# The gate projection as eight groups of split products ahead of the attention's units

## The chip, the cores and the metric

The kernel runs on one core of one Trainium2 chip. The metric is the device time of one execution in microseconds (us). Engines are called TensorE (PE in the profile; PEld are its weight loads), VectorE (DVE), ScalarE (ACT), GpSimd (POOL) and SyncE (SP); the last one here only issues DMA transfers.

## What is computed

A two-layer trunk over 512 positions of width 1024, in float32: a gMLP mixer and a mixture of experts (MoE), then shared keys and values, then a forgetting attention and a second MoE. The change touches the attention alone:

```python
def forgetting_attention(h, k, v, cum, w_qg, q_norm, w_out):
    q, gate = jnp.split(h @ w_qg, 2, axis=-1)
    q = rmsnorm(q.reshape(B, S, N_HEADS, HEAD_DIM), q_norm)
    ...
        s = jnp.einsum('bqhd,bkhd->bhqk', q[:, q0:q1], kb).astype(jnp.float32) * scale
        decay = cum[:, :, q0:q1, None] - cum[:, :, None, :q1]
        s = jnp.where(mask, s + decay, -jnp.inf)
        p = jax.nn.softmax(s, axis=-1)
        outs.append(jnp.einsum('bhqk,bkhd->bqhd', p.astype(vb.dtype), vb))
    ...
    return (o * jax.nn.sigmoid(gate)) @ w_out
```

`h` is 512 x 1024; query and gate are 1024 wide each, 16 heads of 64. The sigmoid is computed as a tanh of half the argument, with the factors folded in elsewhere.

## The kernel before

Every engine has a program written out by hand, in order, and the engines meet at semaphores. Weights of the dense projections come as 20-odd tiles of 1024 rows x 512 columns (2 MB) through a ring of two buffers in `EB[1]`: `load_tile(i)` on SyncE (line 317) waits until the groups of products that read tile i-2 are done. A dense projection is made of *split products* (`split_product`, lines 1067 to 1069): both operands are split into a rounded high part and the rest, and three matmuls (high x high, high x low, low x high) of type float32r take the place of one float32 matmul. The weight tile is split by ScalarE (line 528, high part, four pieces) and VectorE (line 753, low part, in place). One *group* is the 8 x 3 matmuls that fill a PSUM bank of 128 x 512; it increments `acc_ready`. `project_heads` makes the 8 query groups (tiles T_Q, T_Q+1), in banks 0 and 1, and turns normalised heads (`turn_heads`, line 1296) behind each next group; the last turn, `turn_heads(15)`, came alone.

The attention then runs in 32 *units*: 8 pairs of heads (c), each with 4 query blocks of 128 (i), keys up to (i+1) x 128 wide. On TensorE a unit u is: scores of two heads (line 1374) and the mask (1377) into banks 0/1 or 2/3; a quarter of the gate projection of this pair; every fourth unit the output product of the pair before (1402), 16 matmuls; the transposes of the probabilities of unit u-2 (1413). The gate's quarter is two plain float32 products of 128 x 128 by 128 x 512 (line 1389) into bank 7, with raw weights from the ring and with `hT`, which VectorE restores as the sum of the two halves (line 1005) in the first four units. Each float32 product appears as two MATMUL records. `g_done` counts a pair's gate; ScalarE applies tanh (line 696) into `GT` and counts `g_out`.

VectorE in unit u: adds the decay row and takes the maximum for two heads (line 1015; the first needs the row buffers `nck`), reciprocal (1024) and scaling (1028) of unit u-1, copy of the first head's transposes of unit u-2 (1034), and after a pair's output product the gating and its split (1040 to 1042). ScalarE: two exponentials (687), copy of the second head's transposes (705). The row buffers `nck` are loaded by ScalarE's queue (line 674), two pairs at first and then one pair at a time, two pairs ahead.

TensorE's transposes of a unit wait for VectorE's scaling of that unit and for both copies of the unit before it; the scores wait for the maxima two units back; the output product waits for the last copies of its pair and for `o_gated` of the pair before.

Of the kernel before, what the change touches and what calls it, by code (L numbers as in the profile page):

```python
# [24 lines left out]
P = 128  # L25
D = 1024
T = 512
NT = T // P
# [25 lines left out]
def trunk(nc, x_in, a_norm, a_w_in, a_b_in, a_v_norm, a_w_s, a_b_s, a_w_out, kv_norm, kv_w, kv_b_f, k_norm,  # L54
          b_norm, b_w_qg, q_norm, b_w_out, m_norm, m_w_group, m_b_group, m_w_expert, m_b_expert,
          m_w1, m_w3, m_w2, out):
    with ExitStack() as ctx:
# [177 lines left out]
        v_out = sem("v_out")  # L235
        g_done = sem("g_done")
        g_out = sem("g_out")
# [41 lines left out]

        G_V, G_U, G_K, G_VV, G_Q, G_WO = 0, 16, 32, 40, 48, 56  # L280


        def split_no(i):
            return i if i < T_G else i - (T_WO - T_G)


        H_LO = {"a": 0, "kv": 2 * NT, "b": 4 * NT}
        H_BACK = 6 * NT

# [15 lines left out]
        def _(sp):  # L305
            def load_tile(i):
                if i >= 2:

                    j = i - 2
                    if T_O <= j < T_K:  # L310
                        sp.wait_ge(out_done, 4 * (j - T_O + 1))
                    elif j >= T_G:
                        sp.wait_ge(g_done, 4 * (j - T_G + 1))
                    else:
                        groups = 4 * (j + 1 if j < T_O else j + 1 - (T_K - T_O))
                        sp.wait_ge(acc_ready, groups)
                sp.dma_start(ring[i % 2], tiles[i]).then_inc(tile_loaded[i % 2], 16)
# [174 lines left out]
        def _(act):  # L492
# [177 lines left out]
            act.dma_start(ncum_rows, junk[0:HEADS, 0:T]).then_inc(ncum_stored, 16)  # L670
            head_norms(1, G_Q, 1, QT, {1: T_Q + 1})
            def load_nck(c):
# [9 lines left out]
            for u in range(PAIRS * NT + 2):  # L682
                if u < PAIRS * NT:
# [6 lines left out]
                    if u % NT == NT - 1 and u // NT + 2 < PAIRS:  # L690
                        load_nck(u // NT + 2)
                if u < PAIRS * NT and u % NT == NT - 1:

                    c = u // NT
                    act.wait_ge(g_done, c + 1)
                    a.activation(GT[:, c, :], ps[7][:, :], ACT.Tanh, scale=0.5).then_inc(g_out, 1)

                q = u - (PAIRS // 2 * NT + 2)
# [13 lines left out]
        def _(dve):  # L712
# [282 lines left out]
            then(v.tensor_scalar(kq_gain[:, 1:2], kq_gain[:, 1:2], DH ** -0.5, None, ALU.mult))  # L995
            head_norms(1, G_Q, {1: T_Q + 1})
            n_units = PAIRS * NT
            for u in range(n_units + 4):
                if u < n_units:
                    i, c = u % NT, u // NT  # L1000
                    w = (i + 1) * P
                    if c == 0:

                        dve.wait_ge(acc_ready, G_Q + 8)
                        v.tensor_tensor(hT[:, 2 * i:2 * i + 2, :], hT_hi[:, 2 * i:2 * i + 2, :].bitcast(F32),  # L1005
                                        hT_lo[:, 2 * i:2 * i + 2, :].bitcast(F32), ALU.add).then_inc(h_lo, 1)
                    if i == 0:
                        dve.wait_ge(nck_loaded[c % 2], 32 * (c // 2 + 1))
                    for h in range(2):
                        dve.wait_ge(s_done, 2 * u + h + 1)  # L1010
                        if u >= 3:

                            dve.wait_ge(pt_tr, 2 * (u - 3) + h + 1)

                        v.tensor_tensor_reduce(out=Pr[:, u % 3, h, 0:w], in0=ps[2 * (u % 2) + h][:, 0:w],
                                               in1=nck[:, c % 2, h, 0:w], scale=-1.0, scalar=BIG, op0=ALU.add,
                                               op1=ALU.min, accum_out=nmx[:, u % 3, h:h + 1]).then_inc(s_max, 1)
# [44 lines left out]
        def _(pe):  # L1062
# [51 lines left out]

            def project_transposed(i, g0, bank_free):

                for j in range(4):
                    g = g0 + j
                    bank_free(g)
                    for k in range(KD):  # L1120
                        wait_split(i, k, j == 0)
                        last = split_product(ps[g % 2][:, :], w_part(i % 2, k, j * P, (j + 1) * P), h_part(k),
                                             k == 0, k == KD - 1)
                    last.then_inc(acc_ready, 1)

            def router_step(l, t):
# [233 lines left out]
            project_heads("b", T_Q, G_Q, 1, free_q)  # L1360
            turn_heads(15)


            pe.wait_ge(kn_out, 16)
            n_units = PAIRS * NT
            for u in range(n_units + 3):
                if u < n_units:
# [8 lines left out]
                    for h in range(2):  # L1376
                        mm(ps[2 * (u % 2) + h][:, i * P:w], ident_b[:, :], mask_b[:, :], start=False, stop=True)\
                            .then_inc(s_done, 1)

                    j = T_G + c // 4  # L1380
                    if i == 0:
                        pe.wait_ge(tile_loaded[j % 2], 16 * (j // 2 + 1))
                        if c >= 1:
                            pe.wait_ge(g_out, c)
                    if c == 0:

                        pe.wait_ge(h_lo, H_BACK + i + 1)
                    for k in range(2 * i, 2 * i + 2):
                        last = mm(ps[7][:, :], ring[j % 2][:, k, c % 4 * P:(c % 4 + 1) * P], hT[:, k, :],  # L1389
                                  start=k == 0, stop=k == KD - 1)  # L1390
                    if i == NT - 1:
                        last.then_inc(g_done, 1)
                if u >= 3 and (u - 3) % NT == NT - 1:
# [4 lines left out]
                    if c >= 1:  # L1398
                        pe.wait_ge(o_gated, c)
                    for b in range(NT):  # L1400
                        for h in range(2):
# [52 lines left out]
```

## Time and profile before

| | us |
|---|---|
| median of 3 runs | 1839.46 |
| lowest, highest | 1835.39, 1840.23 |
| span of the profiled execution | 1838.5 |
| TensorE busy | 1706.3 (93%) |
| VectorE busy | 640.1 (35%) |
| ScalarE busy | 378.6 (21%) |

The page shows one execution; times in it run from the span's start. Busy times are unions of records, and a matmul's record reaches past the start of the next one, so the rate of a stream of matmuls is read from starts, not from lengths. "Idle before, releaser" says how long an engine stood still before a row and who ended that. Shares over the whole span mix stages; the stage in question is 1062 to 1211.

### The profile page before, as it was taken

Reading aid. Unit: us, or ns where it says so; the run is one execution under the profiler, and the core shown is the slowest. Engines: PE = TensorE matmul, PEld = TensorE weight load, DVE = VectorE, ACT = ScalarE, POOL = GpSimd, SP = SyncE. Lnnn points to the kernel's source line nnn. Section 1 sums busy time; section 2 is a strip of 40 time slices with the busy share of each in tenths; the row PEclk is TensorE's granted clock in tenths of the full one; section 3 lists DMA queues with packets and bytes.
Section 4 is the critical chain, followed back from the end, with each engine's and each line's share of the span. In section 5 each row is a group of like instructions: output and inputs, shape, how many; then the busy total and the mean of one; then the engine's idle time right before and its main releaser. Section 6 shows DMA issues by size and latency. Waiting matters only on the chain.

```text
span 1838.5 us, 22412 instructions
## 1 busy us (share of the span) xinstructions
PE 1706.3 (93%) x8401; PEld 882.0 (48%) x8402; DVE 640.1 (35%) x1174; ACT 378.6 (21%) x685; POOL 35.3 (2%) x62
## 2 busy tenths in 40 slices
PE   6999998899999999997699989987999999999993
PEld 4888887333333333332587844465333333333331
DVE  5336523322222222223725346734322222222223
ACT  5441312011111111111441334512111111111110
POOL 2000000000000000000000000000000000000001
PEclk8999999899999999998789999988999999999997
DMA  5652227799999779994223122055799797999964
GB/s 185 210 183 90 93 92 290 296 405 427 429 428 428 308 299 417 430 416 132 81 92 102 48 80 81 24 227 230 305 424 427 315 389 320 417 427 430 429 271 148
DMA packets 64254, 497.62 MB, mean 271 GB/s; under 512 B 5760, under 2 KB 5872, under 8 KB 39120
## 3 DMA queue, kind: packets, MB, share of 16 engines
q1 hardware_dynamic: 52256, 461.39, 61.6%
q10 hardware_dynamic: 7920, 22.58, 3.3%
q0 software_dynamic: 4032, 13.01, 2.2%
q8 instruction: 32, 0.52, 0.1%
q14 instruction: 14, 0.11, 0.0%
HBM read 468.61 MB, written 28.34 MB: 270 GB/s over the span
## 4 chain that ended last, share of the span: by engine, by line
PE 49%; issue 45%; DVE 4%; DMA 1%; ACT 1%; POOL 1%; POOLq 0%; ACTq 0%; DVEq 0%
PE ps L1193 13%; PE ps L1176 7%; PE ps L1208 7%; PE ps L1067 6%; PE ps L1069 6%; PE ps L1068 6%; DVE SCR L845 1%; PE ps L1183 1%; DVE SCR L735 1%; PE ps L1263 1%; DMA EB<-y_rows,pos_i 1%; DVE X L865 1%; PE ps L1337 1%; POOL EB L450 1%; PE ps L1090 0%
## 5 line engine op out<-in xcount | busy, mean ns | idle before, releaser
L1193 PE MATMUL ps<-EB,SCR 128*64 128x512 f32 x2176 | 478.6, 592 | 2.9 <-DVE SCR L828 2.9
L1193 PEld LDWEIGHTS ps<-EB,SCR 128*64 128x64 f32 x2176 | 157.2, 137 | 311.7 <-issue 308.4
L1176 PE MATMUL ps<-H,SCR 128*64 128x512 f32 x1120 | 255.2, 598 | 7.2 <-DVE SCR L780 7.2
L842 DVE TENSOR_TENSOR SCR<-SCR,ps 64x512 f32<-64x512 f32 x68 | 46.9, 690 | 605.2 <-ACT SCR L566 605.2
L1208 PE MATMUL ps<-EB,SCR 128*64 128x512 f32 x1088 | 248.5, 598 | 0.0
L1069 PE MATMUL ps<-EB_r 128*128 128x512 f32 x512 | 202.4, 395 | 0.0
L572 ACT ACTIVATE SCR<-ps 64x512 f32 (+1 forms) x136 | 80.6, 593 | 545.4 <-PE ps L1208 487.5
L1176 PEld LDWEIGHTS ps<-H,SCR 128*64 128x64 f32 x1120 | 81.9, 138 | 167.7 <-issue 167.7
L1208 PEld LDWEIGHTS ps<-EB,SCR 128*64 128x64 f32 x1088 | 72.5, 136 | 127.6 <-issue 127.6
L1067 PE MATMUL ps<-EB_r,H_r 128*128 128x512 f32 x320 | 129.5, 405 | 1.4 <-DVE EB L882 0.9
L1068 PE MATMUL ps<-EB_r,H_r 128*128 128x512 f32 x320 | 127.4, 398 | 0.0
L1068 PE MATMUL ps<-EB_r 128*128 128x512 f32 x320 | 125.1, 391 | 0.0
L566 ACT ACTIVATE SCR<-ps 64x512 f32<-64x512 f32 x68 | 40.1, 589 | 363.0 <-PE ps L1193 363.0
L753 DVE TENSOR_TENSOR EB_r<-EB,EB_r 128x1024 fp32r<-128x1024 f32 x80 | 92.8, 1220 | 46.9 <-ACT EB_r L528 46.9
L1069 PEld LDWEIGHTS ps<-EB_r 128*128 128x128 f32 x512 | 98.2, 192 | 21.2
L845 DVE COPY SCR<-ps 128x512 f32<-128x512 f32 x68 | 47.0, 692 | 141.7 <-PE ps L1176 141.7
L528 ACT ACTIVATE EB_r<-EB 128x1024 fp32r<-128x1024 f32 x80 | 78.3, 1047 | 82.2 <-DMA EB<-in_a_w_out 44.0
L1067 PE MATMUL ps<-EB_r 128*128 128x512 f32 x192 | 75.7, 394 | 2.0 <-DVE EB_r L1042 2.0
L1389 PE MATMUL ps<-H,EB 128*128 128x512 f32 x128 | 64.3, 625 | 6.4 <-DVE H L1005 5.7
L1067 PEld LDWEIGHTS ps<-EB_r,H_r 128*128 128x128 f32 x320 | 62.1, 194 | 14.9 <-DVE EB L882 1.3
L1068 PEld LDWEIGHTS ps<-EB_r,H_r 128*128 128x128 f32 x320 | 61.9, 193 | 12.6
L1068 PEld LDWEIGHTS ps<-EB_r 128*128 128x128 f32 x320 | 60.5, 189 | 12.6
(199 smaller groups left out, 1377.3 us busy)
## 6 DMA issues: line engine op xcount, KB each, us to landing
EB<-in_m_w SPq DMA_DIRECT2D x192, 2048.0 KB, 10.2
y_rows<-SCR ACTq DMA_DIRECT2D x68, 256.0 KB, 7.5
EB<-in_a_w_in SPq DMA_DIRECT2D x8, 2048.0 KB, 10.4
y_rows<-X SPq DMA_DIRECT2D x4, 2048.0 KB, 14.6
EB<-in_a_w_out SPq DMA_DIRECT2D x4, 2048.0 KB, 7.9
EB<-in_kv_w SPq DMA_DIRECT2D x4, 2048.0 KB, 10.3
EB<-in_b_w_qg SPq DMA_DIRECT2D x4, 2048.0 KB, 10.3
SCR<-ncum_rows ACTq DMA_DIRECT2D x16, 256.0 KB, 3.6
```

The costliest lines, as they stand in the source:

```text
L528: a.activation(ring_hi[j][:, 2 * q:2 * q + 2, :], ring[j][:, 2 * q:2 * q + 2, :], ACT.Copy)\
L572: a.activation(ysb[0:CAP, bass.ds((n & 1) * D + h * COL, COL)], ps[4][h * CAP:(h + 1) * CAP, :], ACT.Copy).then_inc(m["y_out"], 1)
L753: v.tensor_tensor(ring_lo[j][:, 2 * q:2 * q + 2, :], ring[j][:, 2 * q:2 * q + 2, :], ring_hi[j][:, 2 * q:2 * q + 2, :].bitcast(F32), ALU.s ...
L842: v.tensor_tensor(hid[0:CAP, :], silu[CAP:P, :], ps[0][CAP:P, :], ALU.mult).then_inc(m["hid"], 1)
L845: v.tensor_copy(xg, ps[1][:, :]).then_inc(m["xg"], 1)
L1067: mm(o, left[0], right[0], start=start, stop=False)
L1068: mm(o, left[0], right[1], start=False, stop=False)
L1069: return mm(o, left[1], right[0], start=False, stop=stop)
L1176: last = mm(ps[1][h * CAP:(h + 1) * CAP, :], S[:, c, :], H[:, c * D + h * COL:c * D + (h + 1) * COL], start=c == 0, stop=c == NT - 1)
L1193: last = mm(ps[0][h * CAP:(h + 1) * CAP, :], xT[:, k, :], w[:, k, :], start=k == 0, stop=k == KD - 1)
L1208: last = mm(ps[4][h * CAP:(h + 1) * CAP, :], hidT[:, k, :], w2_sb[s][:, k, h * COL:(h + 1) * COL], start=k == 0, stop=k == KE - 1)
L1389: last = mm(ps[7][:, :], ring[j % 2][:, k, c % 4 * P:(c % 4 + 1) * P], hT[:, k, :], start=k == 0, stop=k == KD - 1)
```

## The change

The gate projection leaves the units. It is made of split products like the others, eight groups (`G_G`) in banks 6 and 7 in turn, right behind the query projection, with the last turn of the query heads behind its first group. Its two weight tiles are split by ScalarE and VectorE: the first within `head_norms` at its sixth group, the second by ScalarE behind the first tanh and by VectorE behind `head_norms`. ScalarE's eight tanh stand one behind the other ahead of the first load of `nck`. The sum that restored `hT` is gone from VectorE. SyncE's loads of the two output-projection tiles now wait for gate groups 4 and 8 (`acc_ready`) in place of `g_done`. The first output product waits once for all eight tanh.

```diff
-                    elif j >= T_G:
-                        sp.wait_ge(g_done, 4 * (j - T_G + 1))
                     else:
                         groups = 4 * (j + 1 if j < T_O else j + 1 - (T_K - T_O))
                         sp.wait_ge(acc_ready, groups)
...
-            head_norms(1, G_Q, 1, QT, {1: T_Q + 1})
+            head_norms(1, G_Q, 1, QT, {1: T_Q + 1, 5: T_G})
+            for c in range(PAIRS):
+                act.wait_ge(acc_ready, G_G + c + 1)
+                a.activation(GT[:, c, :], ps[6 + c % 2][:, :], ACT.Tanh, scale=0.5).then_inc(g_out, 1)
+                if c == 0:
+                    split_tile(T_G + 1)
+
...
-                if u < PAIRS * NT and u % NT == NT - 1:
-
-                    c = u // NT
-                    act.wait_ge(g_done, c + 1)
-                    a.activation(GT[:, c, :], ps[7][:, :], ACT.Tanh, scale=0.5).then_inc(g_out, 1)
-
...
-            head_norms(1, G_Q, {1: T_Q + 1})
+            head_norms(1, G_Q, {1: T_Q + 1, 5: T_G})
+            split_tile(T_G + 1)
...
-                    if c == 0:
-
-                        dve.wait_ge(acc_ready, G_Q + 8)
-                        v.tensor_tensor(hT[:, 2 * i:2 * i + 2, :], hT_hi[:, 2 * i:2 * i + 2, :].bitcast(F32),
-                                        hT_lo[:, 2 * i:2 * i + 2, :].bitcast(F32), ALU.add).then_inc(h_lo, 1)
...
-            turn_heads(15)
-
+
+            def free_g(g):
+                c = g - G_G
+                if c >= 2:
+                    pe.wait_ge(g_out, c - 1)
+
+            pe.wait_ge(ncum_ready, 1)
+            project_transposed(T_G, G_G, free_g, 6, lambda: turn_heads(15))
+            project_transposed(T_G + 1, G_G + 4, free_g, 6)
...
-                    j = T_G + c // 4
-                    if i == 0:
-                        pe.wait_ge(tile_loaded[j % 2], 16 * (j // 2 + 1))
-                        if c >= 1:
-                            pe.wait_ge(g_out, c)
-                    if c == 0:
-
-                        pe.wait_ge(h_lo, H_BACK + i + 1)
-                    for k in range(2 * i, 2 * i + 2):
-                        last = mm(ps[7][:, :], ring[j % 2][:, k, c % 4 * P:(c % 4 + 1) * P], hT[:, k, :],
-                                  start=k == 0, stop=k == KD - 1)
-                    if i == NT - 1:
-                        last.then_inc(g_done, 1)
...
+                    else:
+                        pe.wait_ge(g_out, PAIRS)
```

TensorE's order around an output product, before (L1374 scores, L1377 mask, L1389 gate, L1402 output product, L1413 transposes):

```order
L1413 MATMUL ps<-ident,SCR 128x128 x8
L1374 MATMUL ps<-EB 128x384 x2
L1377 MATMUL ps<-mask_b,ident_b 128x128 x2
L1389 MATMUL ps<-H,EB 128x512 x2
L1402 MATMUL ps<-EB 64x512 x2
L1402 MATMUL ps<-EB 64x384 x2
L1402 MATMUL ps<-EB 64x256 x2
L1402 MATMUL ps<-EB 64x128 x2
L1413 MATMUL ps<-ident,SCR 128x128 x2
L1374 MATMUL ps<-EB 128x512 x2
L1377 MATMUL ps<-mask_b,ident_b 128x128 x2
L1389 MATMUL ps<-H,EB 128x512 x2
```

The same place after (L1375 scores, L1378 mask, L1391 output product, L1402 transposes):

```order
L1402 MATMUL ps<-ident,SCR 128x128 x8
L1375 MATMUL ps<-EB 128x384 x2
L1378 MATMUL ps<-mask_b,ident_b 128x128 x2
L1391 MATMUL ps<-EB 64x512 x2
L1391 MATMUL ps<-EB 64x384 x2
L1391 MATMUL ps<-EB 64x256 x2
L1391 MATMUL ps<-EB 64x128 x2
L1402 MATMUL ps<-ident,SCR 128x128 x2
L1375 MATMUL ps<-EB 128x512 x2
L1378 MATMUL ps<-mask_b,ident_b 128x128 x2
```

The gate's rows are gone; scores, output product, transposes and the next scores now follow one another directly.

ScalarE's order between the last query heads and the first exponentials, before (L641, L643 head norms, L655 turned heads out, L674 row loads, L687 exponentials):

```order
L641 ACTIVATE SCR<-ps 128x512
L643 ACTIVATE hr<-hss,eps 128x8
L655 ACTIVATE EB<-ps,cols 128x4x128 x2
L674 DMA SCR<-ncum_rows 128x512 x4
L687 ACT_TABLE_LOAD
L687 ACTIVATE SCR,rsum<-SCR,nmx 128x128 x2
```

The same place after (L637, L639, L651 the heads; L670 tanh; L524 split of the second gate tile; L676 row loads; L689 exponentials):

```order
L637 ACTIVATE SCR<-ps 128x512
L639 ACTIVATE hr<-hss,eps 128x8
L651 ACTIVATE EB<-ps,cols 128x4x128 x2
L670 ACT_TABLE_LOAD
L670 ACTIVATE EB<-ps 128x512
L524 ACTIVATE EB_r<-EB 128x1024 x4
L670 ACTIVATE EB<-ps 128x512 x7
L676 DMA SCR<-ncum_rows 128x512 x4
L689 ACTIVATE SCR,rsum<-SCR,nmx 128x128 x2
```

The row loads and the exponentials now stand behind the eight tanh and a tile's split.

## Rows read from the trace of the kernel before

**Rows 1.** The page, part 1: busy us, share of the span, instructions.
```profile
PE 1706.3 (93%) x8401; PEld 882.0 (48%) x8402; DVE 640.1 (35%) x1174; ACT 378.6 (21%) x685; POOL 35.3 (2%) x62
```

**Rows 2.** The windows view: stretch, length, busy us (instructions) per engine, granted clock.
```profile
core 0: us, PE busy (x) PEld busy (x) DVE busy (x) ACT busy (x) POOL busy (x), PEclk, DMA share, GB/s
1062.80:1074.10 11.30, 4.20 (x22) 1.89 (x20) 2.72 (x5) 3.26 (x5) 0.00 (x0) 1.00 0.85 274
1074.10:1087.80 13.70, 11.87 (x34) 4.86 (x34) 9.63 (x30) 5.60 (x19) 0.00 (x0) 0.75 0.03 10
1087.80:1200.70 112.90, 111.01 (x538) 53.91 (x536) 75.03 (x251) 53.33 (x154) 0.00 (x0) 1.00 0.15 49
1200.70:1210.90 10.20, 5.88 (x24) 3.23 (x24) 3.96 (x9) 4.49 (x5) 0.00 (x0) 0.67 0.59 204
```

**Rows 3.** The timeline, TensorE, one pair of units: start, length, what.
```profile
1112.75 2.38 PE L1402 MATMUL ps<-EB 128*64 128x512 f32 x16
1115.06 0.44 PE L1413 MATMUL ps<-ident,SCR 128*128 128x128 f32 x2
...
1116.61 1.94 PE L1389 MATMUL ps<-H,EB 128*128 128x512 f32 x4
1118.38 0.60 PE L1413 MATMUL ps<-ident,SCR 128*128 128x128 f32 x4
...
1128.60 2.37 PE L1402 MATMUL ps<-EB 128*64 128x512 f32 x16
```

**Rows 4.** The same pair, VectorE, where it waited: idle before, releaser.
```profile
1115.43 0.29 DVE L1034 COPY EB<-ps 128x128 f32<-128x128 f32 x1 [2.62 <-PE ps L1413]
1116.76 0.69 DVE L1015 CUSTOM_DVE_ANT_0 SCR<-ps,SCR 128x512 f32<-128x512 f32 x1 [1.04 <-PE ps L1377]
...
1123.17 0.42 DVE L1015 CUSTOM_DVE_ANT_0 SCR<-ps,SCR 128x256 f32<-128x256 f32 x1 [0.24 <-PE ps L1377]
...
1125.43 0.69 DVE L1034 COPY EB<-ps 128x512 f32<-128x512 f32 x1 [0.89 <-PE ps L1413]
1126.88 0.56 DVE L1015 CUSTOM_DVE_ANT_0 SCR<-ps,SCR 128x384 f32<-128x384 f32 x1 [0.75 <-PE ps L1377]
```

**Rows 5.** The timeline in the u projection, TensorE, 24 split matmuls apart.
```profile
214.02 0.39 PE L1067 MATMUL ps<-H_r,EB_r 128*128 128x512 f32 x1
...
219.46 0.39 PE L1067 MATMUL ps<-H_r,EB_r 128*128 128x512 f32 x1
```

**Rows 6.** The chain that ended last, two turns of heads in the key stage.
```profile
937.92 0.44 PE ps L1296 x4
...
943.86 0.44 PE ps L1296 x4
```

**Rows 7.** The timeline between query projection and units, four engines and queues.
```profile
1062.61 0.54 SPq L317 DMA_DIRECT2D EB<-in_b_w_qg  x1
...
1065.28 0.66 PE L1296 MATMUL ps<-ident,SCR 128*128 128x128 f32 x4 [2.27 <-DVE SCR L960]
...
1066.75 2.12 ACTq L674 DMA_DIRECT2D SCR<-ncum_rows  x4
...
1074.10 0.29 DVE L1015 CUSTOM_DVE_ANT_0 SCR<-ps,SCR 128x128 f32<-128x128 f32 x1 [7.74 <-DMA SCR<-ncum_rows]
```

**Rows 8.** Landing of the row loads: all sixteen; two at 1134, beside a tile load.
```profile
DMA to landing us min/median/max: 3.0/3.6/7.1
...
SCR<-ncum_rows ACTq DMA_DIRECT2D x2, 256.0 KB, 4.6
```

**Rows 9.** Groups by line, 1062 to 1210: count, busy us, mean ns, idle before.
```profile
L753 DVE TENSOR_TENSOR EB_r<-EB,EB_r 128x1024 fp32r<-128x1024 f32 x4 | 4.9, 1220 | 0.0
...
L696 ACT ACTIVATE EB<-ps 128x512 f32<-128x512 f32 x8 | 4.7, 592 | 0.0
```

**Rows 10.** The windows view in steps of 8 us, columns as in rows 2.
```profile
1072.00:1080.00 8.00, 4.20 (x6) 1.67 (x8) 4.03 (x13) 1.97 (x8) 0.00 (x0) 0.69 0.23 89
1264.00:1272.00 8.00, 2.72 (x60) 2.32 (x56) 3.85 (x17) 2.58 (x4) 0.00 (x0) 0.85 1.01 428
```

More of the change, by code:

```diff
@@ L235, in trunk @@
         v_out = sem("v_out")
-        g_done = sem("g_done")
         g_out = sem("g_out")
@@ L278, in trunk @@
         T_V, T_U, T_O, T_K, T_VV, T_Q, T_G, T_WO = 0, 4, 8, 12, 14, 16, 18, 20
-        G_V, G_U, G_K, G_VV, G_Q, G_WO = 0, 16, 32, 40, 48, 56
+        G_V, G_U, G_K, G_VV, G_Q, G_G, G_WO = 0, 16, 32, 40, 48, 56, 64
         def split_no(i):
-            return i if i < T_G else i - (T_WO - T_G)
+            return i
         H_LO = {"a": 0, "kv": 2 * NT, "b": 4 * NT}
-        H_BACK = 6 * NT
         TURN = {"a": 3, "kv": 3, "b": 2}
@@ L1113, in project, with project_transposed @@
                     last.then_inc(acc_ready, 1)
-            def project_transposed(i, g0, bank_free):
+            def project_transposed(i, g0, bank_free, bank=0, after_first=None):
                 for j in range(4):
@@ L1121, in project_transposed @@
                         wait_split(i, k, j == 0)
-                        last = split_product(ps[g % 2][:, :], w_part(i % 2, k, j * P, (j + 1) * P), h_part(k),
+                        last = split_product(ps[bank + g % 2][:, :], w_part(i % 2, k, j * P, (j + 1) * P), h_part(k),
                                              k == 0, k == KD - 1)
                     last.then_inc(acc_ready, 1)
+                    if after_first is not None and j == 0:
+                        after_first()
             def router_step(l, t):
```

## The prediction

> **What bounds the kernel now.** I read the page's first part: TensorE is busy 93% of the span [rows 1], so it bounds the kernel nearly everywhere. The change touches one stage, so I cut that stage out with the windows view [rows 2]. From the end of the query projection to the first unit's maximum, 1062.8 to 1074.1: TensorE 4.2 us busy of 11.3. Attention units, 1087.8 to 1200.7: TensorE 111.0 of 112.9, VectorE 75.0, ScalarE 53.3. Tail, 1200.7 to 1210.9, when the output projection starts.
>
> In the steady units (pairs c, four units i = 0..3 each; "T(i)" the transposes of unit i, "S(i)" its scores, "O" the pair's output product) the timeline of TensorE gives the make-up of one pair [rows 3]: O starts at 1112.75 and again at 1128.60, so a pair takes 15.85 us. The gate holds TensorE from 1116.61 to the next T at 1118.38, 1.77 us, and much the same in the other three units: about 7.2 us. What is left, O (2.31) with the S, their masks and the T, is 8.6.
>
> VectorE's timeline of the same pair [rows 4] is the one to read for what comes next. It waits five times: 2.62 (copy of T(0), behind O), 1.04 (scores 512 wide), 0.24, 0.89 and 0.75, in all 5.54. So it works 15.85 - 5.54 = 10.31 us a pair, more than TensorE without the gate: the bound changes hands.
>
> **The gate ahead of the units (added).** 64 split products of three matmuls each. The same form stood in the u projection: 24 matmuls from 214.02 to 219.46, 5.44 us a group [rows 5]. Eight groups: 43.5 us, plus the turn of the last query heads that now falls behind the first group, about 0.4: 44 us, from 1062.8 to 1106.8, all on the path. The wait in which TensorE sat idle for that turn (2.27 us, [rows 7]) is hidden by the first group; it lies inside the 11.3 us that I replace below, so it is not counted again.
>
> Both tiles must be split in time. The first one loads when four query groups are done, as now, and is split at the sixth group; the key stage did just that (a tile split at the same place) and its turns stayed 5.94 us apart, 937.92 to 943.86 [rows 6], so I price it at nothing. The second is issued at 1062.61 [rows 7]; give it 11 us to land, to 1073.6. ScalarE and behind it VectorE split it in four pieces, 1.22 each on VectorE, 4.9 in all [rows 9]: ready by about 1079, wanted at 1085. If that cover went, each us of lateness would be one on the path. Banks 6 and 7 need tanh two groups back; tanh of the second group waits behind that split, to about 1078.9, and TensorE asks for it at 1079.6. It holds by less than a us.
>
> **The first maximum (a wait moved and lengthened).** The row buffers of the decay are loaded by ScalarE, and this issue now stands behind all eight tanh. Behind it are queued the first exponentials; VectorE's first maximum waits for the data, and TensorE, after two units' scores, for VectorE. The last gate group ends at 1106.8; who waits for it moves 0.2 later, as SyncE's issue at 1062.61 behind the last query group of 1062.4 [rows 7], one tanh is 0.59 [rows 9], so the issue comes at 1107.6 to 1107.7. Before, from the issue at 1066.75 to the first maximum at 1074.10 took 7.35 us [rows 7], beside the 2 MB tile load of 1062.61. Lower bound: the second row's issue, 0.45 after the first, and the median landing of 3.6 [rows 8], so 1111.8. Upper: 7.35 again, 1115.1. A tile load stands beside it again, since the last tile is issued when the last gate group frees its buffer, but it no longer has a lead of 4 us. A pair of row loads issued with such a load beside it landed in 4.6 [rows 8]. I take 1113.7, **39.6 us later** than 1074.10.
>
> What the Trainium skill says of it (page "DMA: Bandwidth & Descriptors", section on queues, rings and completion order): a DMA engine takes the rows it has work for in turn, a packet at a time. By that rule both transfers share from the start, and by it the start would lie in the upper half of my bounds, 1 us later at most.
>
> **The gate out of the units (removed).** With 7.2 us of TensorE gone the pair does not fall to TensorE's 8.6. Take VectorE's work, 10.31, and ask which waits stay.
> - 0.24, 0.89, 0.75: VectorE waited for scores or transposes that stood behind a gate product. Without it TensorE has them ready. Gone.
> - 1.04: from T(0)'s start, 1115.06, S(3) follows at once, and the 512-wide scores reach VectorE at 1116.76; the gate is not in this chain. Stays.
> - 2.62: O starts once the copies of the 512-wide T(3) are out, then 2.31 of O and 0.37 of T(0) must pass before the copy of T(0). VectorE began unit 2's maxima at 1126.88 - 15.85 = 1111.03 and had work until 1115.43 - 2.62 = 1112.81 [rows 4]: 1.78. O, held back by a gate product, began only 1.72 after those maxima, at 1112.75. Now it begins as soon as the copies are out, about 0.25 after them, and the copy of T(0) can start 0.25 + 2.31 + 0.37 = 2.93 after them. 2.93 - 1.78 = 1.15 stays. S(2) stands in the same queue and adds about 0.15.
> A pair: 10.31 + 1.04 + 1.15 + 0.15 = **12.65, say 12.7**. Bounds: 10.3 (no wait) and 14.0 (10.31 + 2.62 + 1.04).
>
> Sum from the first maximum to the output projection. First pair, 1074.10 to 1087.8 [rows 2]: 13.7 now. After: VectorE's work without the steps that the first units skip is some 6.5, and the waits for S(2) and S(3) at the lower clock, which follows the idle stretch, about 2.5: 9, with 7 and 12 as ends. Seven pairs: 112.9 now; 7 x 12.7 = 88.9, plus the split of the output tile, four pieces of 1.22 on VectorE [rows 9], of which one falls in the 1.15 wait: +3.7, together 92.6. Tail: 10.2 both times [rows 2]; its chain of copies, O and gating has no gate product. So 136.8 becomes 9 + 92.6 + 10.2 = 111.8, **25.0 us less**. Tanh and the sum of the two query-side halves (L1005) leave the units too; ScalarE waits there anyway, and the latter lies in the first pair.
>
> Net: +39.6 - 25.0 = +14.6. The output projection and the MoE behind it start that much later with their loads issued by the same releases, so nothing is won back. The profiled span of 1838.5 lies 1.0 under the median of the runs; 1838.5 + 14.6 + 1.0 = **1854**.
>
> **Rivals.**
> (1) TensorE's clock. It now would be busy two thirds of a pair with gaps of 2 us, and the first pair begins after 5 to 6 idle us. Before, after such a stretch, the granted clock was 0.69 in the window from 1072 [rows 10], that is for part of it 1.2 GHz instead of 2.4, and over the first pair 0.75 [rows 2]; it rose when TensorE had been dense. Against: a window with TensorE 2.72 busy of 8 had 0.85 [rows 10]. If it stays low through the units, TensorE needs 2 x 8.6 = 17.2 a pair, 4.5 over my 12.7, in seven pairs +31: **1885**; if half the time, 1870. The Trainium skill ("TensorE: Matmul & The Clock Gate", section on PSUM-queue depth-cycling) describes it: frequent micro-idles between groups of matmuls made the clock go up and down. By that rule the time would be that of this rival.
> (2) VectorE never waits: a pair costs 10.3, the sum falls by 7 x 2.4 = 16.8: **1837**, no change. It decides where O and S(3) hide behind VectorE's work; against it stands the order of O, T(0), S(3) on TensorE.
> (3) Faster: the units stay TensorE's and fall to its own 8.6 a pair: 7 x 4.1 = 29 less than my sum, **1825**. The break-even is a pair of 12.7 - 14.6/7 = 10.6, and faster by 0.3% needs under 9.8. VectorE's measured work of 10.31 excludes it, unless a part of it is waiting that the trace shows as work.
>
> **How the numbers follow.** 0.3% is 5.5 us, about what measurement tells from no change. Forecast, 12 to 14 us a pair and the first maximum within its bounds: 1848 to 1865, chance 0.74. Clock rival 0.14, from 1865 to 1885. VectorE without waits 0.09, 1837 to 1845. Faster 0.03. The range takes in the forecast and the nearer side of both neighbours: 1845 to 1868. Faster 0.03, same 0.09, slower 0.88.
>
> **What would show it.** In the profile of the changed kernel: TensorE full from 1062.8 to about 1107, in groups of 5.44; then idle till a first VectorE maximum near 1114, with a DMA as releaser; pairs 12.7 apart, O to O, with VectorE waiting about 1.0 before the 512-wide maximum and 1.2 before the copy of T(0), and hardly elsewhere; clock 1.00 from the second pair on; output projection at 1225 or so. I am wrong if pairs take under 11.3 (waits were mis-read), over 14 (clock), or if the groups of the gate stall for a tile.

## The result, and the profile after

| | before | changed |
|---|---|---|
| median of four runs, us | 1838.75 | 1864.78 |
| lowest, highest | 1835.39, 1840.23 | 1863.42, 1865.98 |
| span of the profiled execution | 1838.5 | 1861.6 |
| mean granted clock of TensorE | 0.963 | 0.954 |
| output projection starts at | 1210.9 [rows 2] | 1234.6 |

The changed kernel is slower: ratio 1.0141, 95% interval 1.0127 to 1.0156, or 26.0 us. The forecast was 14.6 us slower. The time lies inside the range, but more than 10 us above the forecast, and that difference is what most of the experiments are about.

The page's first part of the changed kernel, to be held against [rows 1]:

```profile
PE 1710.4 (92%) x8465; PEld 904.0 (49%) x8466; DVE 644.0 (35%) x1178; ACT 385.8 (21%) x693; POOL 34.8 (2%) x62
```

TensorE is busy 4 us longer, which says nothing of the 23. The output projection starts 23.7 us later than before, and the span is 23.1 us longer: the whole change lies in this one stage. Here is the stage in the windows view, with the columns of [rows 2]; the stretches are the gate, the idle stretch behind it, the first pair up to the first row of steady work, the other units, and the tail.

```profile
core 0: us, PE busy (x) PEld busy (x) DVE busy (x) ACT busy (x) POOL busy (x), PEclk, DMA share, GB/s
1062.80:1107.10 44.30, 44.30 (x200) 36.47 (x198) 6.21 (x7) 11.41 (x16) 0.00 (x0) 1.00 0.29 95
1107.10:1115.40 8.30, 1.64 (x13) 0.83 (x12) 0.04 (x1) 0.60 (x1) 0.00 (x0) 0.85 0.82 260
1115.40:1122.70 7.30, 5.48 (x24) 2.35 (x24) 6.11 (x27) 4.99 (x18) 0.00 (x0) 0.70 0.38 138
1122.70:1224.10 101.40, 78.95 (x420) 42.77 (x420) 74.57 (x252) 48.66 (x146) 0.00 (x0) 0.77 0.10 32
1224.10:1234.60 10.50, 6.35 (x24) 3.48 (x24) 3.81 (x7) 4.63 (x6) 0.00 (x0) 0.61 0.11 27
```

The gate is as forecast: 44.3 us, TensorE busy in all of it, clock 1.00. In the fourth stretch TensorE is busy 78% where it had been busy 98%, VectorE only 74%, and the granted clock is 0.77 where [rows 2] had 1.00. So no engine is full there, and the clock is low.

The timeline of the same kernel from the end of the gate, four engines and queues (start, length, what, idle before and releaser); it answers to [rows 7]:

```profile
1107.28 0.38 SPq L313 DMA_DIRECT2D EB<-in_b_w_out  x1
1107.29 0.60 ACT L670 ACTIVATE EB<-ps 128x512 f32<-128x512 f32 x1 [4.84 <-PE ps L1061]
1107.35 2.02 ACTq L676 DMA_DIRECT2D SCR<-ncum_rows  x4
...
1115.36 0.29 DVE L1007 CUSTOM_DVE_ANT_0 SCR<-ps,SCR 128x128 f32<-128x128 f32 x1 [36.42 <-DMA SCR<-ncum_rows]
1115.92 1.65 PE L1375 MATMUL ps<-EB 64*128 64x384 f32 x4 [7.18 <-DVE nmx L1007]
...
1234.61 0.50 PE L1059 MATMUL ps<-EB_r 128*128 128x512 f32 x1 [1.97 <-DVE EB_r L1034]
```

The row loads are issued at 1107.35, 0.07 us behind a 2 MB tile load, and the first maximum comes 8.0 us after the issue. TensorE stands idle for 7.18 us.

TensorE's timeline in one pair of the changed kernel, from one output product to the next; it answers to [rows 3]:

```profile
1128.09 2.38 PE L1391 MATMUL ps<-EB 128*64 128x512 f32 x16
...
1132.90 0.29 PE L1378 MATMUL ps<-mask_b,ident_b 128*128 128x128 bf16 x2
1134.74 0.84 PE L1402 MATMUL ps<-ident,SCR 128*128 128x128 f32 x6 [1.55 <-DVE EB L1026]
1135.52 0.70 PE L1375 MATMUL ps<-EB 64*128 64x256 f32 x4
1136.15 0.28 PE L1378 MATMUL ps<-mask_b,ident_b 128*128 128x128 bf16 x2
1138.40 1.94 PE L1402 MATMUL ps<-ident,SCR 128*128 128x128 f32 x8 [1.97 <-DVE EB L1026]
1140.27 1.65 PE L1375 MATMUL ps<-EB 64*128 64x384 f32 x4
1141.86 0.39 PE L1378 MATMUL ps<-mask_b,ident_b 128*128 128x128 bf16 x2
1142.18 3.07 PE L1391 MATMUL ps<-EB 128*64 128x512 f32 x16
```

The same two groups of instructions before, where no gap stood ahead of them:

```profile
1124.79 1.04 PE L1413 MATMUL ps<-ident,SCR 128*128 128x128 f32 x8
1125.76 0.92 PE L1374 MATMUL ps<-EB 64*128 64x384 f32 x4
```

This is the heart of the result. A pair takes 14.09 us, not 12.7. TensorE waits twice, 1.55 us ahead of T(2) and 1.97 us ahead of T(3), each time for VectorE's copies. In this pair T(3), behind the second gap, takes 1.94 us where it took 1.04, the scores 384 wide 1.65 for 0.92, and the output product 3.07 for 2.38. Per 8 us the windows view shows it as clock 1.00 and then 0.57:

```profile
1128.00:1136.00 8.00, 6.45 (x46) 3.40 (x44) 5.84 (x19) 3.46 (x10) 0.00 (x0) 1.00 0.16 45
1136.00:1144.00 8.00, 6.04 (x25) 3.00 (x24) 5.88 (x24) 4.16 (x14) 0.00 (x0) 0.57 0.06 23
```

This pair does not stand for all of them. In five of the eight pairs the clock is low already at T(2), which then takes 1.08 to 1.51 us where it takes 0.84 at full clock. Two of the five:

```profile
1163.75 1.20 PE L1402 MATMUL ps<-ident,SCR 128*128 128x128 f32 x6 [1.55 <-DVE EB L1026]
...
1208.41 1.47 PE L1402 MATMUL ps<-ident,SCR 128*128 128x128 f32 x6 [1.55 <-DVE EB L1026]
```

So the low level begins near either gap, once in each pair.

VectorE's waits around the end of that pair, to be held against [rows 4]:

```profile
1142.18 0.56 DVE L1007 CUSTOM_DVE_ANT_0 SCR<-ps,SCR 128x384 f32<-128x384 f32 x1 [1.96 <-PE ps L1378]
...
1145.55 0.29 DVE L1026 COPY EB<-ps 128x128 f32<-128x128 f32 x1 [1.59 <-PE ps L1402]
1146.88 0.69 DVE L1007 CUSTOM_DVE_ANT_0 SCR<-ps,SCR 128x512 f32<-128x512 f32 x1 [1.04 <-PE ps L1378]
```

Two of these were forecast, 1.15 and 1.04. The first, 1.96 for the slow T(3) and scores, was not. The product starts lie 14.09, 14.79, 14.12, 16.38, 14.29 and 13.90 us apart (the fourth pair holds the split of the output tile). Before they lay 15.84, 15.85, 15.83, 16.43, 15.84 and 15.75 apart.

### The profile page after: what moved, and what is told of

Same layout as the page of the kernel before. It is cut to its first block, busy times and chain, and to the rows that moved or that the text cites. A ratio compares the mean times of both kernels' runs of the same rounds, so it can differ in the third digit from the quotient of the medians.

```text
span 1861.6 us, 22546 instructions
## 1 busy us (share of the span) xinstructions
PE 1710.4 (92%) x8465; PEld 904.0 (49%) x8466; DVE 644.0 (35%) x1178; ACT 385.8 (21%) x693; POOL 34.8 (2%) x62
## 4 chain that ended last, share of the span: by engine, by line
PE 48%; issue 45%; DVE 4%; DMA 1%; ACT 1%; POOL 1%; POOLq 0%; ACTq 0%; DVEq 0%
PE ps L1187 13%; PE ps L1170 7%; PE ps L1202 7%; PE ps L1059 6%; PE ps L1061 6%; PE ps L1060 6%; DVE SCR L841 1%; PE ps L1177 1%; DVE SCR L731 1%; PE ps L1257 1%; DMA EB<-y_rows,pos_i 1%; DVE X L861 1%; PE ps L1331 1%; POOL EB L446 0%; PE ps L1082 0%
## 5 line engine op out<-in xcount | busy, mean ns | idle before, releaser
L1061 PE MATMUL ps<-EB_r 128*128 128x512 f32 x512 | 202.1, 395 | 0.0
L1060 PE MATMUL ps<-EB_r 128*128 128x512 f32 x384 | 150.0, 391 | 0.0
L749 DVE TENSOR_TENSOR EB_r<-EB,EB_r 128x1024 fp32r<-128x1024 f32 x88 | 102.1, 1220 | 56.2 <-ACT EB_r L524 56.1
L1061 PEld LDWEIGHTS ps<-EB_r 128*128 128x128 f32 x512 | 97.7, 191 | 20.9
L524 ACT ACTIVATE EB_r<-EB 128x1024 fp32r<-128x1024 f32 x88 | 86.0, 1047 | 81.0 <-DMA EB<-in_a_w_out 43.9
L1060 PEld LDWEIGHTS ps<-EB_r 128*128 128x128 f32 x384 | 72.5, 189 | 15.0
L1059 PE MATMUL ps<-EB_r 128*128 128x512 f32 x192 | 75.6, 394 | 2.0 <-DVE EB_r L1034 2.0
L1059 PE MATMUL ps<-H_r,EB_r 128*128 128x512 f32 x192 | 75.1, 391 | 0.0
L1061 PE MATMUL ps<-H_r,EB_r 128*128 128x512 f32 x192 | 74.7, 389 | 0.0
L1059 PEld LDWEIGHTS ps<-EB_r,H_r 128*128 128x128 f32 x320 | 61.9, 193 | 14.7 <-DVE EB L878 1.3
## 6 DMA issues: line engine op xcount, KB each, us to landing
EB<-in_m_w SPq DMA_DIRECT2D x192, 2048.0 KB, 10.2
EB<-in_b_w_qg SPq DMA_DIRECT2D x4, 2048.0 KB, 10.2
```

The lines of the kernel that those rows point to most:

```text
L524: a.activation(ring_hi[j][:, 2 * q:2 * q + 2, :], ring[j][:, 2 * q:2 * q + 2, :], ACT.Copy)\
L749: v.tensor_tensor(ring_lo[j][:, 2 * q:2 * q + 2, :], ring[j][:, 2 * q:2 * q + 2, :], ring_hi[j][:, 2 * q:2 * q + 2, :].bitcast(F32), ALU.s ...
L1059: mm(o, left[0], right[0], start=start, stop=False)
L1060: mm(o, left[0], right[1], start=False, stop=False)
L1061: return mm(o, left[1], right[0], start=False, stop=stop)
```

## The experiments

The theory: the sum is right at the full clock, and the lost clock in the units and the late rows make up the rest. The rivals: the chain between VectorE and TensorE is longer than read, so that pairs take 14 us at any clock; or the share of work on TensorE, not the gaps, sets the clock. Ratios are against the kernel before on the same chip, whose medians were 1838.71 for the first four kernels, 1839.23 for the next four and 1837.51 for the last two.

**Filler in both gaps.** Eight extra matmuls of type float32r, 128 x 512, stand ahead of T(2) and ahead of T(3) in each pair. They write into bank 7, which is free there, and nobody reads the result.

```diff
                 if 2 <= u < n_units + 2:
                     q = u - 2
                     i, c = q % NT, q // NT
+                    if u == 2:
+                        pe.wait_ge(g_out, PAIRS)
+                    if u % NT in (0, 1):
+                        for _ in range(8):
+                            mm(ps[7][:, :], hT_hi[:, 0, 0:P], hT_hi[:, 1, :], start=True, stop=True)
```

> The changed kernel, and in its attention units eight more float32r matmuls of 512 columns (8 x 0.227 = 1.8 us, results into free bank 7, read by nobody) ahead of the transposes in units 0 and 1 of every pair, where TensorE waits 2 us for VectorE's copies. Theory (lost clock): pairs took 14.3 us instead of the 12.7 forecast because the granted clock was 0.57 to 0.90; with the gaps filled it stays at 1.00, pairs fall to 12.7, and the whole is 8 to 11 us shorter than the changed kernel, 1854 to 1857. Rival (the recurrence was mis-sized, the clock is harmless): pairs stay at 14.3 or grow, time 1865 or more.

Measured: 1852.27 us (1848.68 to 1855.1), ratio 1.0077 (1.0057 to 1.0096). Extra work made the changed kernel 12.5 us faster, somewhat more than the 8 to 11 expected. Pairs: 12.38, 12.36, 12.38, 15.51, 12.38, 12.37. The windows view over the units of this kernel, and VectorE's waits in a pair:

```profile
1130.00:1218.00 88.00, 84.30 (x514) 51.71 (x512) 71.41 (x237) 45.32 (x136) 0.00 (x0) 1.00 0.10 31
```

```profile
1142.90 0.56 DVE L1007 CUSTOM_DVE_ANT_0 SCR<-ps,SCR 128x384 f32<-128x384 f32 x1 [0.38 <-PE ps L1378]
...
1145.52 0.29 DVE L1026 COPY EB<-ps 128x128 f32<-128x128 f32 x1 [0.85 <-PE ps L1407]
1146.85 0.69 DVE L1007 CUSTOM_DVE_ANT_0 SCR<-ps,SCR 128x512 f32<-128x512 f32 x1 [1.04 <-PE ps L1378]
```

The clock is 1.00 and the wait of 1.96 is down to 0.38. The three waits left come to 2.27 us; the forecast had 2.34 (1.04 + 1.15 + 0.15). A pair of 12.38 stands beside the forecast's 12.65. So the rival of a longer chain falls. The sum of the waits was right, its terms less so: 0.85 stands for 1.15, and 0.38 of a wait that the forecast called gone is still there.

From the first maximum (1117.29) to the output projection (1223.89) 106.6 us pass, 12.6 less than in the changed kernel. Of these 9.9 lie in the seven pairs (101.4 and 91.5 us) and 2.7 in the tail, which takes 7.8 us at clock 1.00. The kernel before had the tail at 10.2 us and 0.67 [rows 2], so part of what the filler wins is nothing that the change had lost.

**Half the filler** (four in place of eight, both places).

> As the run before with half the filling, four matmuls (0.9 us) at the same two places. Lost clock: it holds the clock in part, time between the changed kernel's 1865 and that of the full filling, some 1858 to 1862. Rival: no difference from 1865, or up to 1 us.

Measured: 1854.21 (1852.15 to 1855.45), ratio 1.0087 (1.007 to 1.0104). Pairs of 12.4 to 12.7, and 15.89 with the split; clock 0.98 in the units. The interval overlaps that of eight; I had expected a part of the gain, 1858 to 1862, and it came nearly whole.

**A quarter of it** (two, that is 0.45 us at each place).

> The changed kernel with two filling matmuls (0.45 us) at each of the two places in a pair, where four and eight gave pairs of 12.4 us at a clock of 1.00. If the clock follows how busy TensorE is, pairs lie between 12.4 and 14.3 and the time between 1854 and 1865, about 1860. If any filling is enough, 1854.

Measured: 1853.21 (1850.63 to 1854.81), ratio 1.0077 (1.0062 to 1.0092). Pairs: 12.37, 12.38, 12.37, 15.51, 13.13, 12.38. The windows view over the units, first this kernel, then the changed kernel without filler:

```profile
1128.00:1216.00 88.00, 67.22 (x424) 35.50 (x424) 71.56 (x237) 45.17 (x135) 0.00 (x0) 0.98 0.10 31
```

```profile
1128.00:1216.00 88.00, 68.26 (x364) 36.41 (x364) 64.65 (x215) 41.91 (x124) 0.00 (x0) 0.77 0.10 31
```

TensorE's busy share is the same or lower (67.2 against 68.3 of 88 us), and the clock is 0.98 against 0.77. That alone does not refute the rival of too little work, because slow matmuls count as busy for longer: this kernel did 424 matmuls in the 88 us, the other 364. It shows that the busy share cannot tell whether the clock holds. It also shows that the gaps need not be closed. They are only shorter, 1.03 and 1.45 us, and T(3) runs at full clock behind the second:

```profile
1146.97 0.85 PE L1407 MATMUL ps<-ident,SCR 128*128 128x128 f32 x6 [1.03 <-DVE EB L1026]
...
1150.63 1.06 PE L1407 MATMUL ps<-ident,SCR 128*128 128x128 f32 x8 [1.45 <-DVE EB L1026]
```

This kernel does not yet say which gap matters.

**Four in one gap only**, ahead of T(2) (unit 0 of the next pair, in the words of the expectation) or ahead of T(3) (unit 1). The first of the two edits, shown against the kernel with eight fillers:

```diff
-                    if u % NT in (0, 1):
-                        for _ in range(8):
+                    if u % NT in (0,):
+                        for _ in range(4):
```

> The changed kernel with four filling matmuls (0.9 us) in unit 0 of a pair alone: the amount per pair is that of two plus two, which kept pairs at 12.4, but the gap ahead of unit 1's transposes stays open. If the amount of work decides the clock, pairs stay at 12.4 and the time is near 1853. If each gap counts, that pair's clock falls again and the time lies at 1857 to 1865.

> The same four matmuls in unit 1 of a pair alone, the gap ahead of unit 0's transposes open. By amount: near 1853, as with the other place. If one of the gaps is the one that counts, this run and the one before differ, one near 1853 and one near 1860 or more.

Measured ahead of T(2): 1863.25 (1862.48 to 1863.6), ratio 1.0139 (1.0116 to 1.0163), no gain over the changed kernel; pairs 13.78, 14.1, 14.26, 17.28, 14.16, 14.16. Ahead of T(3), in `(1,)`: 1855.37 (1854.69 to 1858.89), ratio 1.0102 (1.0075 to 1.013), and pairs 12.76, 12.38, 12.37, 15.51, 12.37, 12.72. The units in the windows view, and TensorE's gap that was left, ahead of T(2) first:

```profile
1128.00:1216.00 88.00, 71.83 (x386) 37.80 (x384) 64.12 (x215) 42.00 (x126) 0.00 (x0) 0.83 0.09 31
```

```profile
1136.54 1.94 PE L1407 MATMUL ps<-ident,SCR 128*128 128x128 f32 x8 [1.97 <-DVE EB L1026]
```

and ahead of T(3):

```profile
1128.00:1216.00 88.00, 69.78 (x424) 38.95 (x421) 71.14 (x237) 45.43 (x135) 0.00 (x0) 0.93 0.09 31
```

```profile
1159.49 0.85 PE L1407 MATMUL ps<-ident,SCR 128*128 128x128 f32 x6 [1.55 <-DVE EB L1026]
```

The gap of 1.97 us, left alone, keeps the clock at 0.83, and T(3) at its slow 1.94 in three of seven pairs and partly slow in three more. The gap of 1.55 us, left alone, still goes with 0.93 and pairs of 12.4 to 12.8. The gap ahead of T(3) carries most of the loss (by the ratios 0.39 of the 0.54 per cent that four fillers in both gaps gave back; the interval of this run is wide, and its upper end reaches into that of the changed kernel). Here the rival "share of work" falls: these two kernels and the one with two fillers in each gap have the same four fillers in a pair, and their clocks are 0.83, 0.93 and 0.98.

Part of the difference is not in the clock but in what it slows. In the second kernel T(2) is sometimes slow too:

```profile
1199.74 1.06 PE L1407 MATMUL ps<-ident,SCR 128*128 128x128 f32 x6 [1.55 <-DVE EB L1026]
```

The pair in which this stands takes 12.72 us, 0.35 more than one at full clock; it shows again as a longer wait of VectorE at its end (0.73 for 0.38). In the first kernel the pair with the slow T(3) shown takes 13.78, 1.4 more. A low clock behind T(2) is nearly hidden behind VectorE's work, and one at T(3), the scores and O is not.

**The row loads ahead of the tanh.**

```diff
             head_norms(1, G_Q, 1, QT, {1: T_Q + 1, 5: T_G})
...
+            act.wait_ge(ncum_stored, 16)
+            act.wait_ge(kn_out, 16)
+            load_nck(0)
+            load_nck(1)
             for c in range(PAIRS):
                 act.wait_ge(acc_ready, G_G + c + 1)
...
-            act.wait_ge(ncum_stored, 16)
-
-            act.wait_ge(kn_out, 16)
-            load_nck(0)
-            load_nck(1)
             for u in range(PAIRS * NT + 2):
```

> The changed kernel with the first two pairs' row loads issued by ScalarE ahead of the eight tanh in place of behind them. Theory (the wait of 8 us before the first maximum is this queueing): first maximum about 0.8 us after the last gate group, at 1108 in place of 1115.4, no idle stretch of 7 us on TensorE, first pair at full clock: 8 to 10 us shorter, about 1856. Rival (the units are bound by something that starts later, or the gate's own splits suffer): under 4 us.

Measured: 1852.8 (1851.78 to 1854.1), ratio 1.0078 (1.0061 to 1.0095): 12.0 us less than the changed kernel, where 8 to 10 were expected. VectorE's first maximum in the timeline:

```profile
1108.84 0.29 DVE L1006 CUSTOM_DVE_ANT_0 SCR<-ps,SCR 128x128 f32<-128x128 f32 x1 [28.12 <-PE ps L1377]
```

It is 6.5 us earlier, and its releaser is now the scores and no longer a DMA. Pairs stay at 13.9 to 14.2 (16.36 with the split) and the clock of the units at 0.78, so this loss is separate from the clock's. In the profiled executions the output projection starts 9.8 us earlier (1224.80): 6.5 from the maximum and 3.3 behind it. Of the latter, 2.3 lie ahead of the first output product: from the first maximum to there it is 10.5 us at clock 1.00, where the changed kernel took 12.7 at 0.70 behind its idle stretch. The spans differ by 9.3 and the medians by 12.0; the rest is scatter between executions, since the profiled one is the fastest of its four in the changed kernel and the slowest of its four here.

**Both together**, rows ahead and eight fillers.

> Both edits at once. If the two losses are separate they add up: 16 to 20 us shorter than the changed kernel, 1845 to 1849, still slower than the kernel before by 6 to 10: that remainder is 44 us of gate ahead against what its absence saves in the units at full clock. Rival (either edit repairs the clock alone): 8 to 11 us shorter.

Measured: 1842.8 (1842.01 to 1846.13), ratio 1.0024 (1.0014 to 1.0034); pairs 12.38, clock 1.00, output projection at 1214.41. That is 22.0 of the 26.0 us back, nearly the 12.5 + 12.0 of the two alone. What is left is 4.1 us: the first maximum comes at 1108.42, 34.3 us later than before, and from there to the output projection it takes 106.0 us where it took 136.8, 30.8 less. The difference is 3.5. That is not yet the bare exchange of one place of the gate for the other, since the kernel before has neither its rows early nor a tail at full clock. Beside the kernel before with its first rows early (1833.41, below) this one is 9 to 10 us slower.

**The kernel before, four sums first.** All four sums that restore `hT` (L1005) stand ahead of the first maximum, in its wait for the rows.

```diff
-                    if c == 0:
-
-                        dve.wait_ge(acc_ready, G_Q + 8)
+                    if u == 0:
+                      dve.wait_ge(acc_ready, G_Q + 8)
+                      for i in range(NT):
                         v.tensor_tensor(hT[:, 2 * i:2 * i + 2, :], hT_hi[:, 2 * i:2 * i + 2, :].bitcast(F32),
                                         hT_lo[:, 2 * i:2 * i + 2, :].bitcast(F32), ALU.add).then_inc(h_lo, 1)
+                      i = 0
```

> The kernel before, with VectorE's four sums that restore the float32 rows (line 1005) all ahead of the first maximum instead of one in each of the first four units. VectorE waits 7.7 us there for the row loads anyway, and TensorE waited 5.75 us for the second sum and then ran its first pair at a clock of 0.75. Theory (that idle stretch and its clock cost 10 us in the kernel before, which no gate ahead is needed to win): 7 to 10 us faster than before, about 1830. Rival (the row loads bind the first pair anyway): within 3 us of before.

Measured: 1834.82 (1831.06 to 1838.53), ratio 0.998 (0.9971 to 0.9989), 4.4 us less than before. The first output product came at 1091.63 in place of 1096.91. The sign holds; I had expected 7 to 10.

**The kernel before, first rows early.** The halves of the row buffer are exchanged, so that the first pair's rows do not have to wait for the turned heads, and are loaded ahead of the query heads.

```diff
-            head_norms(1, G_Q, 1, QT, {1: T_Q + 1})
...
-                    act.dma_start(nck[:, c % 2, h, :], ncum_rows[2 * c + h].partition_broadcast(P))\
+                    act.dma_start(nck[:, (c + 1) % 2, h, :], ncum_rows[2 * c + h].partition_broadcast(P))\
...
             act.wait_ge(ncum_stored, 16)
+            load_nck(0)
+            head_norms(1, G_Q, 1, QT, {1: T_Q + 1})
...
             act.wait_ge(kn_out, 16)
-            load_nck(0)
             load_nck(1)
...
-                                               in1=nck[:, c % 2, h, 0:w], scale=-1.0, scalar=BIG, op0=ALU.add,
+                                               in1=nck[:, (c + 1) % 2, h, 0:w], scale=-1.0, scalar=BIG, op0=ALU.add,
```

> The kernel before, with the two halves of the row buffer swapped, so that the first pair's rows lie where the query heads keep nothing, and their load is issued ahead of the query heads' work instead of behind it. First maximum at about 1067.6 in place of 1074.1, no idle stretch on TensorE: 7 to 10 us faster than before, about 1830. Rival (TensorE's first units wait for the sums of line 1005 as long as before): under 3 us.

Measured: 1833.41 (1829.19 to 1835.34), ratio 0.9971 (0.9961 to 0.9981), 5.8 us less than before, so faster than both kernels, but under the 7 to 10 expected. The windows view of its first pair, with the columns of [rows 2]:

```profile
1062.80:1067.20 4.40, 1.43 (x11) 1.08 (x12) 2.71 (x4) 1.68 (x4) 0.00 (x0) 1.00 0.73 199
1067.20:1087.70 20.50, 20.37 (x84) 9.21 (x83) 15.45 (x53) 11.34 (x33) 0.00 (x0) 1.00 0.32 112
```

The first maximum is at 1067.2 in place of 1074.1, and the clock stays at 1.00 where [rows 2] had 0.75. The profiled execution is the fastest of its runs; in it the output projection started 10.2 us earlier (1200.68), more than the median gives.

**Both edits to the kernel before.**

> Both edits on the kernel before. They remove the same idle stretch, so they don't add: 7 to 11 us faster than before. Rival (separate losses): 14 or more.

Measured: 1833.33 (1831.0 to 1834.54), ratio 0.997 (0.9958 to 0.9981). That is 5.9 us less than before, where 7 to 11 were expected, and it is no more than the early rows give by themselves. They don't add: once the rows are early there is no such wait left for the sums to hide in. The profiled executions differ in one thing more. The window from 1064 to 1072, this kernel, and then that with the early rows alone:

```profile
1064.00:1072.00 8.00, 6.53 (x21) 3.04 (x21) 5.59 (x9) 3.10 (x7) 0.00 (x0) 0.57 0.90 294
```

```profile
1064.00:1072.00 8.00, 6.23 (x28) 2.84 (x28) 5.90 (x16) 4.49 (x11) 0.00 (x0) 1.00 0.95 300
```

The clock is 0.57 here and 1.00 there, although TensorE stood idle ahead of the last turn of heads for 2.27 and 2.26 us, and ahead of the first scores for 0.78 in both. The slow matmuls begin at 1064.69, before the sums can hold anything up, so this difference is not the edit's; the medians are the same.

## Why the prediction was right in its direction and 10 us short

- **The gate ahead: right.** 44.3 us from 1062.8 to 1107.1 against 44. The first tile's split, the second's, and the last turn behind the first group cost nothing, as priced.
- **The first maximum: 1.7 us short.** Forecast 1113.7, measured 1115.36, outside my upper bound of 1115.1 by 0.3. The issue came at 1107.35, 0.3 earlier than reckoned, so the wait was 8.0 us and not 7.35 at most. It was 7.9 to 8.2 us in all six profiled executions with this order of issues, so it is no accident of one. The bound treated the old wait as the worst case although there the tile load had begun 4 us before the rows. With both issued together the four row loads landed in a median of 8.0 us (5.8 to 9.4); issued 7.2 us behind a tile load, in the run with the rows ahead of the tanh, in 4.0 (3.2 to 4.5). The runs show what was avoidable in it: there the first maximum came 6.5 us sooner.
- **The first pair: 1.6 us too long.** 7.3 to 7.4 against 9; inside its ends. It takes as much off the miss of the pairs (below).
- **The pairs: the step that failed.** The sum of the waits that stay was right at full clock: 12.38 against 12.65 with the filler. The step that failed is the assumption under it, "clock 1.00 from the second pair on". Removing the gate did not only take 7.2 us of work off TensorE, it left gaps of 1.55 and 1.97 us per pair where there had been none, and at one or the other the clock fell in every pair. From the first output product to the seventh it took 87.6 us where my terms give 6 x 12.7 + 3.7 = 79.9: 7.7 too few. The rival of a low clock thus held in part. I gave it 0.14, and priced it by TensorE's work alone (twice 8.6 a pair). In fact nearly half of the time was at the lower level (a mean of 0.77 means 0.46 of it at half speed), and it added 1.7 to the pair shown (14.09 against 12.38), most of it in one wait of VectorE, where the rival's price for half of the time would be about 2.2. The price of half of it, 1870, was nearer to the result of 1864.8 than my forecast of 1854 was.
- **The rule weighed in the prediction.** What the Trainium skill says on its page "TensorE: Matmul & The Clock Gate", in the section on PSUM-queue depth-cycling, is that frequent micro-idles between groups of matmuls make the clock go up and down. This trace agrees: 1.00 and 0.57 in neighbouring windows. I had that section and the low clock behind an idle stretch [rows 10] before me, and leaned on a window with 2.72 busy of 8 at 0.85 as the case against. That window says nothing of gaps that come back in each pair.
- **The output tile's split: right in size.** With the filler that pair was 3.1 longer than its neighbours against 3.7.
- **The sum at full clock: near, in part by luck.** With the filler the median is 13.6 us over before, against my 14.6. In its profiled execution 106.6 us passed from the first maximum to the output projection, 5.2 less than the forecast's 111.8: 1.7 in the first pair, 1.1 in the seven pairs, 2.4 in the tail, which the forecast had left at its low clock. Against that the first maximum came at 1117.29, 3.6 later than forecast, and 2.0 of these the execution had lost ahead of the stage. Counted from the end of the query projection, that run gives about 11 us over before, and not 14.6.
- **The offset between span and median.** 3.2 us in place of 1.0: 2.2 us of the miss. Every execution's time is 1.8 above its span; the rest is that the profiled one was the fastest of the changed kernel's four and that of the kernel before, by its span, the slowest. Nothing in the trace of one execution can show it.

The parts of the miss: +1.7 (first maximum), +7.4 (from there to the output projection: -1.7 in the first pair, +8.8 in the seven pairs, +0.3 in the tail), -0.6 (behind it), +2.2 (offset), together 10.7, which is 1864.8 less the unrounded forecast of 1854.1. By the run with eight fillers the low clock costs 9.9 in the seven pairs; the forecast pair, a little too long, hides 1.1 of it.

What stays open: what makes the clock fall at one of the two gaps in one pair and at the other in the next. At T(3) a gap of 1.45 us, with one of 1.03 ahead of T(2), left the clock at 1.00 in the pair shown, and a gap of 1.97, with one of 0.56, did not; but the shorter gap also had more work ahead of it, and no run varied the one without the other. Nor did a run use filler of another kind, so that it closes a gap and that it is a dense float32r matmul are not told apart. That gate products inside the units, as split products, might give both the short groups and a full TensorE wasn't tried: the low halves of the rows share their memory with the transposed probabilities.

## What to carry to other kernels

Work taken out of the bounding engine's chain is only worth what the next chain lets through: here 7.2 us of TensorE's work a pair were removed and the pair, at full clock, got 3.5 shorter, while the same work cost 44 us elsewhere. When a change leaves short, recurring gaps on TensorE, price the lower clock as a term of the sum, and try two matmuls of filler in each gap before anything else; two in the longest alone was not tried, and four there won back less. Where a stage begins with a wait for a small load, look at what stands ahead of its issue; moving that one issue gave 12.0 us to the changed kernel and 5.8 us to the one before.

## What the runs showed of the hardware that was not expected

- 0.45 us of filler at each of two places made a stretch with TensorE no busier by the records than without it (67.2 and 68.3 of 88 us) run at clock 0.98 and not 0.77, and the kernel 11.6 us faster.
- Where the filler stands matters more than how much it is: two in each gap gave 0.98; four ahead of T(3) gave 0.93 and 7 us by the ratios (1.0102 against 1.0141); the same four ahead of T(2) gave 0.83 and no gain that can be told from none.
- The share of low clock does not price it: a pair with the low clock at T(2) took 0.35 us more, one with it at T(3) 1.4 to 1.7 more.
- The same gap of 2.27 us ahead of the last turn of heads was followed by a low clock in one execution (0.57 over 8 us) and by none in two others, 2.26 us ahead of it in one (1.00) and 2.27 in the kernel before [rows 2] and [rows 7]. So a gap of this size can bring the low clock and need not.
- Small row loads issued at the same time as a 2 MB tile load were usable 8.0 us after the first issue, where the sixteen such loads of the kernel before landed in a median of 3.6 [rows 8].
